# Six neighbouring slots of two down projections by seven products, sums of weights on GpSimd

## The reference, cut to what matters

```
def swiglu(h, w_in, w_out):                # D_FF = 2816
    gu = h @ w_in                          # (256, 1024) @ (1024, 5632)
    g, u = gu[..., :D_FF], gu[..., D_FF:]
    return (jax.nn.silu(g) * u) @ w_out    # (256, 2816) @ (2816, 1024)

for l in range(DEPTH):
    x = x + 0.5 * swiglu(rmsnorm(x, norm_ffn1[l]), ffn1_w_in[l], ffn1_w_out[l])
    z = rmsnorm(x, norm_mix[l]) @ mix_w_in[l]
    ...                                    # S5 state space group and gMLP group
    x = x + y @ mix_w_out[l]
    x = x + 0.5 * swiglu(rmsnorm(x, norm_ffn2[l]), ffn2_w_in[l], ffn2_w_out[l])
return rmsnorm(x, norm_final)
```

## Time and profile before

| | us |
|---|---|
| median of 3 runs | 908.01 (907.7 to 908.34) |
| the profiled execution's own time | 908.17 |
| its span, first to last instruction | 906.4 |
| TensorE busy | 898.2 (99%) |
| VectorE, ScalarE, GpSimd busy | 610.1, 503.6, 371.0 |
| granted TensorE clock, mean | 0.998 of full |

### The profile page before, as it was taken

One profiled execution on the slowest core, in us unless ns is written; L12 is line 12 of the kernel. 1 busy time (PEld: TensorE's weight loads), 2 busy tenths in 40 slices (PEclk: granted clock), 3 DMA queues, 4 the chain that ended last, 5 costly groups with the idle time before them and its releaser, 6 DMA issues.

```text
span 906.4 us, 12861 instructions
## 1 busy us (share of the span) xinstructions
PE 898.2 (99%) x4941; PEld 743.9 (82%) x4941; DVE 610.1 (67%) x713; ACT 503.6 (56%) x735; POOL 371.0 (41%) x574
## 2 busy tenths in 40 slices
PE   8999999999999999999999999999999999999997
PEld 7888888888878888888888888888888888888886
DVE  4555665458976569866965656653888855799577
ACT  6545454458766456545464445445677654656454
POOL 3488999894510000000055889988734100000000
PEclk9999999999999999999999999999999999999999
DMA  9786555544256667755558666555344466786561
GB/s 277 203 266 188 186 186 172 174 165 142 95 190 200 203 202 261 245 203 201 187 173 247 186 188 186 186 186 186 119 161 142 138 219 197 235 283 209 184 217 47
DMA packets 137005, 173.02 MB, mean 191 GB/s; under 512 B 18664, under 2 KB 109936, under 8 KB 136944
## 3 DMA queue, kind: packets, MB, share of 16 engines
q1 hardware_dynamic: 136656, 171.67, 59.1%
q10 hardware_dynamic: 288, 0.53, 0.2%
HBM read 171.13 MB, written 1.05 MB: 190 GB/s over the span
## 4 chain that ended last, share of the span: by engine, by line
PE 99%; DMA 0%; ACT 0%; DVE 0%; issue 0%; SPq 0%; ACTq 0%
PE bank L483 30%; PE bank L485 30%; PE bank L484 30%; PE bank L588 2%; PE bank L493 1%; PE bank L815 1%; DMA raw<-in_ffn_w_in 0%; PE bank L843 0%; PE bank L833 0%; PE bank L856 0%; PE bank L698 0%; PE bank L919 0%; PE bank L705 0%; PE bank L871 0%; PE bank L538 0%; PE bank L881 0%
## 5 line engine op out<-in xcount | busy, mean ns | idle before, releaser
L1306 DVE TENSOR_TENSOR w_lo<-raw,w_hi 128x1024 fp32r<-128x1024 f32 x282 | 356.1, 1272 | 214.1 <-ACT w_hi L998 213.9
L998 ACT ACTIVATE w_hi<-raw 128x1024 fp32r<-128x1024 f32 x282 | 296.6, 1061 | 238.9 <-PE bank L485 226.9
L483 PE MATMUL bank<-w_hi,x_hi 128*128 128x512 f32 x856 | 336.7, 393 | 0.0
L485 PE MATMUL bank<-w_hi,x_lo 128*128 128x512 f32 x856 | 333.4, 390 | 0.0
L484 PE MATMUL bank<-w_lo,x_hi 128*128 128x512 f32 x856 | 333.2, 389 | 0.0
L483 PEld LDWEIGHTS bank<-w_hi,x_hi 128*128 128x128 f32 x856 | 160.7, 188 | 35.5 <-issue 2.5
L485 PEld LDWEIGHTS bank<-w_hi,x_lo 128*128 128x128 f32 x856 | 160.7, 188 | 33.8
L484 PEld LDWEIGHTS bank<-w_lo,x_hi 128*128 128x128 f32 x856 | 160.8, 188 | 32.3
L1646 POOL TENSOR_TENSOR rstd_c<-ms_c,neg_half 128x2 f32<-128x2 f32 (+1 forms) x7 | 6.7, 964 | 395.4 <-DVE ms_c L1349 395.4
L483 PE MATMUL bank<-w_hi,h_hi 128*128 128x512 f32 (+1 forms) x295 | 115.7, 392 | 0.0
L485 PE MATMUL bank<-w_hi,h_lo 128*128 128x512 f32 (+1 forms) x295 | 114.3, 388 | 0.0
(11 more groups left out here) (215 smaller groups left out, 847.6 us busy)
## 6 DMA issues: line engine op xcount, KB each, us to landing
raw<-in_ffn_w_in SPq DMA_DIRECT2D x172, 512.0 KB
raw<-in_ffn_w_out SPq DMA_DIRECT2D x34, 1024.0 KB
raw<-in_mix_w_in SPq DMA_DIRECT2D x12, 1024.0 KB
sums_b<-in_ffn_w_out SPq DMA_DIRECT2D x20, 512.0 KB, 7.1
raw<-in_mix_w_out SPq DMA_DIRECT2D x8, 1024.0 KB
raw<-in_ffn_w_out SPq DMA_DIRECT2D x10, 512.0 KB
raw<-in_ffn_w_out SPq DMA_DIRECT2D x10, 256.0 KB
raw<-in_ffn_w_in SPq DMA_DIRECT2D x8, 256.0 KB, 4.8
```

The source lines that it names most:

```text
L483: mm(o, hi_a, hi_b, start=first, stop=False)
L485: return mm(o, lo_a, hi_b, start=False, stop=last)
L998: A(w_hi[:, n % RING, :], raw[:, s, (n % 2) * 1024:(n % 2) * 1024 + 1024], ACT.Copy).then_inc(hi_done, 1)
L1306: TT(w_lo[:, n % RING, :], raw[:, s, (n % 2) * 1024:(n % 2) * 1024 + 1024], w_hi[:, n % RING, :].bitcast(F32), ALU.subtract).then_inc(lo_d ...
```

## The change

- SEVEN becomes (3, 4, 5, 6, 7, 8): slot 5 is computed by seven products too, so it has sums of activations, sums of weights, and loads three of its four blocks for the ring.
- `sums_make` goes from VectorE's list to GpSimd's: all six sums of a layer stand in a row behind `mix(l)`, each waiting for its own load.
- The areas for the weight sums become four: the two of `sums_b`, each used twice in a layer, and two over `x_hi` and `x_lo` (the input of the up projection, free when that is done) for slots 7 and 8. AREA says which sum lies where.
- Load steps: the first two come one load earlier (26, 28 for 28, 30), the last two at steps 52 and 54 with a wait of SyncE for the end of the up projection, where one at 62 was.
- The splits of the weight sums are at steps 28, 31, 55, 57, 59, 61 for 28, 31, 55, 57, 61.
- To make room `xg` (used at the very end) lies over `s_lo`.

```
-SEVEN = (3, 4, 6, 7, 8)
+SEVEN = (3, 4, 5, 6, 7, 8)
-LOAD_AT = (28, 30, 36, 38, 4 * UB + 18)
-SUMS_AT = (26, 29, 36, 41, 4 * UB + 15)
-SPLIT_AT = (28, 31, 4 * UB + 11, 4 * UB + 13, 4 * UB + 17)
+AREA = (0, 1, 0, 1, 2, 3)
+LOAD_AT = (26, 28, 36, 38, 4 * UB + 8, 4 * UB + 10)
+SPLIT_AT = (28, 31, 4 * UB + 11, 4 * UB + 13, 4 * UB + 15, 4 * UB + 17)
...
+        with ExitStack() as second_use:
+            areas = [second_use.enter_context(nc.sbuf_tensor(f"area{t}", [P, 2048], F32))[:, :] for t in range(2)]
         x_hi = sb("x_hi", [P, KT, L], F32R)
         x_lo = sb("x_lo", [P, KT, L], F32R)
+        areas = [sums_b[:, 0, :], sums_b[:, 1, :]] + areas
...
@@ load_sums (SyncE)
-                        if m > 1:
+                        if i in (2, 3):
                             sp.wait_ge(slo_done, m - 1)
+                        if i > 3:
+                            sp.wait_ge(half_done, half(l, DN2))
...
@@ VectorE
-            def sums_make(l, h):
-                for i in range(N7):
-                    if SUMS_AT[i] == h:
-                        ...
@@ GpSimd
+            def sums_make(l):
+                for i in range(N7):
+                    m = l * N7 + i
+                    q = areas[AREA[i]].rearrange("p (i m) -> p i m", i=4)
+                    pool.wait_ge(*sums_full(m))
+                    nc.gpsimd.tensor_tensor(q[:, T1, :], q[:, 0, :], q[:, T1, :], ALU.subtract).then_inc(sb_done, 1)
+                    pool.wait_ge(sb_done, 4 * m + 1)
+                    nc.gpsimd.tensor_tensor(q[:, T3, :], q[:, 0, :], q[:, 2, :], ALU.subtract).then_inc(sb_done, 1)
+                    pool.wait_ge(sb_done, 4 * m + 2)
+                    nc.gpsimd.tensor_tensor(q[:, T2, :], q[:, 2, :], q[:, T1, :], ALU.subtract).then_inc(sb_done, 1)
+                    pool.wait_ge(sb_done, 4 * m + 3)
+                    nc.gpsimd.tensor_tensor(q[:, T4, :], q[:, 3, :], q[:, T2, :], ALU.subtract).then_inc(sb_done, 1)
...
             mix(0)
+            sums_make(0)
             norm(norm_no(1, 0))
...
             mix(1)
+            sums_make(1)
```

More of the change, by code:

```diff
@@ L184, in build @@
         s_hi = sb("s_hi", [P, 2, 2048], F32R)
+        with ExitStack() as last_use:
+            xg = [last_use.enter_context(nc.sbuf_tensor(f"xg{t}", [P, D], F32)) for t in range(2)]
         s_lo = sb("s_lo", [P, 2, 2048], F32R)
-        hs_lo = sb("hs_lo", [P, 5, 512], F32R)
+        hs_lo = sb("hs_lo", [P, 6, 512], F32R)
+        hs_hi_last = sb("hs_hi_last", [P, 512], F32R)
         sums_b = sb("sums_b", [P, 2, 2048])
         gfin = sb("gfin", [P, D])[:, :]
-        xg = [sb("xg0", [P, D]), sb("xg1", [P, D])]
+        pad = sb("pad", [P, 1024])
         a21 = sb("a21", [P, 2, P])
@@ L269, in build @@
         sb_done, p1_done, fold_done = sem("sb_done"), sem("p1_done"), sem("fold_done")
-        s_full = [sem(f"s_full{i}") for i in range(2)]
+        s_full = [sem(f"s_full{i}") for i in range(4)]
         shi_done, slo_done, seven_done = sem("shi_done"), sem("slo_done"), sem("seven_done")
@@ L289, in gain_out_of, with hs_hi_of, sums_full @@
             return gains[:, g:g + 1]
+        def hs_hi_of(i):
+            return hs_hi[:, i, :] if i < 5 else hs_hi_last[:, :]
+        def sums_full(m):
+            i = m % N7
+            uses = [q for q in range(N7) if AREA[q] == AREA[i]]
+            return s_full[AREA[i]], ((m // N7) * len(uses) + uses.index(i) + 1) * 32
         def turned(pair, k):
@@ L365, in load_sums @@
                             sp.wait_ge(half_done, half(l, UP2) + 1)
-                        if m > 1:
+                        if i in (2, 3):
                             sp.wait_ge(slo_done, m - 1)
+                        if i > 3:
+                            sp.wait_ge(half_done, half(l, DN2))
                         k = 2 * SEVEN[i]
                         src = a["ffn2_w_out"][l, k * P:(k + 2) * P, :].rearrange("(t p) m -> p t m", p=P)
-                        dst = sums_b[:, m % 2, :].rearrange("p (t c m) -> p t c m", t=2, c=2)
+                        dst = areas[AREA[i]].rearrange("p (t c m) -> p t c m", t=2, c=2)
                         for c in range(2):
-                            sp.dma_start(dst[:, :, 1 - c, :], src[:, :, c * 512:c * 512 + 512]).then_inc(s_full[m % 2], 16)
+                            sp.dma_start(dst[:, :, 1 - c, :], src[:, :, c * 512:c * 512 + 512]).then_inc(s_full[AREA[i]], 16)
             def load_ffn(l, j):
@@ L722, in seven_rows @@
                 for q in range(4):
-                    a_hi.append(hs_hi[:, i, q * P:q * P + P])
+                    a_hi.append(hs_hi_of(i)[:, q * P:q * P + P])
                     a_lo.append(hs_lo[:, i, q * P:q * P + P])
@@ L975, in sums_split @@
                             act.wait_ge(seven_done, m - 1)
-                        A(s_hi[:, m % 2, :], sums_b[:, m % 2, :], ACT.Copy).then_inc(shi_done, 1)
+                        A(s_hi[:, m % 2, :], areas[AREA[i]], ACT.Copy).then_inc(shi_done, 1)
             def split(l, h):
@@ L1076, in sums_hi @@
                 act.wait_ge(sa_done, 3 * m + 3)
-                A(hs_hi[:, m % N7, :], sums_a.rearrange("p i m -> p (i m)"), ACT.Copy).then_inc(sahi_done, 1)
+                A(hs_hi_of(m % N7), sums_a.rearrange("p i m -> p (i m)"), ACT.Copy).then_inc(sahi_done, 1)
             def first_product(l, j):
@@ L1329, in sums_split @@
                         dve.wait_ge(shi_done, m + 1)
-                        TT(s_lo[:, m % 2, :], sums_b[:, m % 2, :], s_hi[:, m % 2, :].bitcast(F32), ALU.subtract).then_inc(slo_done, 1)
+                        TT(s_lo[:, m % 2, :], areas[AREA[i]], s_hi[:, m % 2, :].bitcast(F32), ALU.subtract).then_inc(slo_done, 1)
             def residual(l, acc, pair, last_half, c, t, scale):
@@ L1433, in sums_lo @@
                 dve.wait_ge(sahi_done, m + 1)
-                TT(hs_lo[:, m % N7, :], sums_a.rearrange("p i m -> p (i m)"), hs_hi[:, m % N7, :].bitcast(F32),
+                TT(hs_lo[:, m % N7, :], sums_a.rearrange("p i m -> p (i m)"), hs_hi_of(m % N7).bitcast(F32),
                    ALU.subtract).then_inc(salo_done, 1)
@@ L1470, in ffn @@
                         sums_split(l, h)
-                        sums_make(l, h)
                     if j and h - 1 in HIDDEN_AT and HIDDEN_AT.index(h - 1) in SEVEN:
```

## The result

| | us |
|---|---|
| median of the changed kernel, 13 runs | 909.98 (909.18 to 911.89) |
| median of the kernel before, 13 runs beside it | 908.35 (907.70 to 909.22) |
| ratio | 1.0020, interval 1.0013 to 1.0028 |
| profiled execution, time and span | 910.60 and 908.9 |

The change costs 1.6 us. The page's line of busy times, to hold against the earlier trace rows: six matmuls fewer, GpSimd 87 us more.

The account below looks back on a forecast made before the run. TensorE, busy 99% of the span, was taken as the bound. Span 906.4 - 1.36 + 2 x 1.5 = 908.1, plus 1.7 gives 909.8, so a median of 909.6 us; range 906.4 to 911.1.

Parts of the forecast that it names:

- Slot 5 by seven products: TensorE, slot 5: three matmuls less in each layer at 0.227 us, 1.36 us off the path in all.
- Sums of activations: Steps 38 and 39, beside the up projection: extra copies, subtractions and a split, several us ahead of use; cost 0.
- sums off VectorE: Weight sums leaving VectorE, five times four subtractions of 0.69 us per layer, not on the path; gain 0.
- six slots in a row: s_hi and s_lo need 4.4 us, TensorE asks after 6.8 us; cost 0 if nothing else is on VectorE.
- SyncE's wait: SyncE's wait for the end of the up projection is met at 396.06 and holds nothing up; cost 0.
- The loads: Added DMA loads: slot 7's sums land at about 400.4, slot 8's at about 405.4; cost 0.
- The turns: In front of slot 3, GpSimd's subtractions delay VectorE's w_lo and hs_lo: 1.0 to 2.1 us per layer, 1.5 taken.
- Sum: Whole run: span 906.4 - 1.36 + 2 x 1.5 = 908.1, with 1.7 around it 909.8; median 909.6.
- A: Rival: no collision on the path in front of slot 3; time 906.65 us; chance 0.20.
- B: Rival: full turns in front of slot 3, 1.1 us at w_lo and 1.0 at hs_lo per layer; 910.9 us; chance 0.26.
- C: Rival: w_lo meets slot 8's last subtraction, hs_lo none; 0.3 to 0.9 us per layer, 907.2 to 908.4; chance 0.12.

Follow-up runs that it names:

- the kernel with added reads: The kernel before plus eight GpSimd subtractions that serve nothing, in each layer across the chain in front of slot 3: 914.14 us, ratio 1.0061.
- The five-slot kernels: The kernel before with only its weight sums moved to GpSimd: 913.62 us; the same with the first two sums loaded earlier, at steps 26 and 28: 910.37 us.
- writes: The kernel before plus twelve GpSimd memsets that serve nothing and only write, in front of slot 3: 908.36 us, ratio 1.0005.
- blocks first: The changed kernel with blocks 9 and 10 of the transposed activations split ahead of half 50: 906.35 us, ratio 0.9980.
- seven slots: The changed kernel with blocks 9 and 10 split first, and slot 2 by seven products too: 908.00 us, ratio 0.9995.

## Why the prediction was right, step by step

- *Slot 5 by seven products, 1.36 us won.* Right: 4.76 us for the slot, and every kernel with six slots and no stall is 1.25 to 2.1 us under before.
- *Sums of activations, sums off VectorE, six slots in a row, SyncE's wait: 0.* Right together: with the sums on VectorE all of these are present and the kernel takes 907.16 us.
- *The loads.* GpSimd began slot 7's sums at 402.87, which is 401.7 on before's clock (this span runs 1.2 us late at that point); I had 400.4, so that landing, an estimate, was 1.3 us short. Slot 8's began at 409.08, that is 407.9; I had 407.3. GpSimd went on to them as soon as slot 7's were done, so their own landing doesn't show. The error left two subtractions still ahead when w_lo came, as the sum had it, and hs_lo met one in either case.
- *The turns, 1.0 to 2.1 us per layer, middle 1.5.* The term: 1.53 and 1.09, so 2.6 us for 3.0. The turn in front of hs_lo was 1.09 us in each layer (I took 1.0), that at w_lo 0.43 and 0 us (I took a mean of 0.5). The first is mechanism, the second in part luck: at w_lo the turn is 0 to 0.98 us in the traces of this study, by where in a subtraction w_lo falls, and landings estimated to a microsecond couldn't tell where. Those two instructions are shown to be the cost, to within the 0.4 us below: keep GpSimd's sums out of that stretch and 3.0 us come back (909.98 to 907.02, beside medians of before of 908.35 and 908.41), put nothing but reads there and before gets the stall.
- *Sum.* 908.1 for the span (by its own terms 908.04), 907.7 by the terms as measured (906.4 - 1.36 + 2.62); on the medians 1.63 us against 1.6 predicted and 1.26 by the traced terms. The 0.4 between the last two is inside the interval (1.2 to 2.5 us). That the median met the forecast to 0.1 us is partly luck again.
- *The rivals.* A (no collision on the path) is what four kernels of the study became, within 0.6 us of the 906.65 worked out for it. B (both turns full) shows in the kernel with added reads, 0.98 and 1.08 us at the two instructions and a stop of 1.96 us a layer, in its profiled execution. C didn't occur.
- *Nearly missed.* That sums on GpSimd are slow enough to matter in the up projection as well, unless loaded earlier, is nowhere in the prediction, which took the earlier load steps as given. The five-slot kernels showed it.

The rule of the Trainium skill that the prediction set beside its rows ("SBUF — State Buffer", Who interferes with whom: two SBUF inputs on VectorE against a GpSimd instruction that reads, not one that only writes) is borne out on both sides: beside reads w_lo goes from 1.76 to 2.74 us, beside writes it stays at 1.76. The narrower note of the Trainium skill, "Advanced Engine Details and Errata", Mode Summary, which names two-port modes alone, isn't enough to plan with: by it alone w_lo would have stayed at 1.76 us beside reads too.

## What to carry to other kernels

Before work goes to an idle engine, ask what it shares with the engine it leaves, and look for chains with no slack in the stretch where it will run, not at the busy share: here 5.5 us of free GpSimd time cost 1.1 to 1.5 us because they lay across 3.5 us of VectorE work that TensorE was waiting for. A chain without slack costs nothing in the profile until something touches it, so take the slack back first (splitting two blocks one step earlier was enough), then move the work. The saving was three matmuls a layer, 0.68 us, and a single turn in front of hs_lo cost 1.09.

## What was not expected of the hardware

The prediction had read from the earlier trace rows that a waiting GpSimd instruction goes ahead; what it couldn't know is how regular this is. A queued GpSimd subtraction gets its turn between two VectorE instructions that follow each other without a gap: hs_lo, issued 0.1 us before w_lo ended, lost 1.08 to 1.09 us in both layers of all four kernels here in which a GpSimd subtraction was waiting (the changed one, reads, blocks first, seven slots). VectorE never got two turns in a row there. A GpSimd subtraction of 128x512 thus takes 1.30 us alone and up to 2.90 us behind a w_lo of 1536 columns.
